# A hybrid decoder step on one core: pooling sums spread over the projection, pages loaded from SyncE, zero products at the start, and a separate first buffer between the expert passes

## The reference

```python
q, g, cmp_r, sel_r, win_r, u = project(x, norm1_g, w_in, q_norm_g, k_norm_g)
# rmsnorm(x) @ w_in; q and two of the keys are normalised per head of 64
kc, vc = compress(...)             # 32-token blocks of cmp rows through gelu(rows @ w1) @ w2
o = gated sum of compressed, selected-block and window attention
d = trailing_mean(u, w) - u        # w = 2, 4, 8, 16 for four groups of 128 channels
y = (d @ pool_w) * pool_scale      # one 128 x 128 map per group: the "mix"
h = x + concat(o, y) @ w_out
out = h + peer_ffn(rmsnorm(h))     # 16384 single-neuron experts, top 16 of each of 8 heads
```

## Time and profile before

| what | value |
|---|---|
| device time, median of 3 runs | 1684.33 us (1682.02 to 1684.73) |
| the profiled execution: time, span | 1685.28 us, 1683.6 us |
| mean granted TensorE clock | 0.992 |
| busy: PE, DVE, ACT, POOL | 1636.4, 1382.9, 754.5, 516.3 us |
| project: first and last product of PE | 7.12 us, 128.5 us |
| attend: first product of PE | 139.32 us |
| experts: first u unit, first v unit | 503.58 us, 1136.37 us |

### The profile page before, as it was taken

One profiled execution on the slowest core, in us unless ns is written; L12 is line 12 of the kernel. 1 busy time (PEld: TensorE's weight loads), 2 busy tenths in 40 slices (PEclk: granted clock), 3 DMA queues, 4 the chain that ended last, 5 costly groups with the idle time before them and its releaser, 6 DMA issues.

```text
span 1683.6 us, 29916 instructions
## 1 busy us (share of the span) xinstructions
PE 1636.4 (97%) x10496; PEld 1564.9 (93%) x10496; DVE 1382.9 (82%) x2831; ACT 754.5 (45%) x1423; POOL 516.3 (31%) x473
## 2 busy tenths in 40 slices
PE   7997999999999999999999999999999999999999
PEld 7985766689999999999999999999999999999999
DVE  5482456777889999999999989867998899999996
ACT  4331354453224334666666668733333333333332
POOL 3423222100001333322322343342443444444440
PEclk9997999999999999999999999999999999999999
DMA  7626233223226888888988899998999999999994
GB/s 233 209 79 187 76 99 108 78 70 113 64 76 201 286 303 317 290 322 302 330 319 317 304 341 345 361 386 312 354 390 342 366 386 402 398 393 395 401 394 143
DMA packets 187720, 454.20 MB, mean 270 GB/s; under 512 B 25666, under 2 KB 92098, under 8 KB 187106
## 3 DMA queue, kind: packets, MB, share of 16 engines
q1 hardware_dynamic: 111282, 242.78, 40.8%
q0 software_dynamic: 50272, 182.23, 29.5%
q10 hardware_dynamic: 26016, 27.27, 4.7%
HBM read 401.14 MB, written 54.47 MB: 271 GB/s over the span
## 4 chain that ended last, share of the span: by engine, by line
PE 61%; DVE 4%; DMA 3%; issue 1%; ACT 0%; SPq 0%; DVEq 0%; ACTq 0%; POOLq 0%
PE ps L2128 10%; PE ps L2124 10%; PE ps L2123 10%; PE ps L2152 9%; PE ps L2158 9%; PE ps L2155 9%; PE ps L2174 5%; DMA sb_ring<-expert_v 3%; DVE sb_w_lo L1953 1%; DVE sb_slot L1990 1%; DMA sb_scores<-expert_v,sb_row_expert 0%; DVE sb_rows_y L2085 0%; ACT sb_w_hi L1858 0%; DVE sb_hot L1989 0%; DVE sb_hot L1986 0%
## 5 line engine op out<-in xcount | busy, mean ns | idle before, releaser
L1858 ACT ACTIVATE sb_w_hi<-sb_ring 128x1024 fp32r<-128x1024 f32 x254 | 269.5, 1061 | 506.5 <-PE ps L2158 231.7
L1953 DVE TENSOR_TENSOR sb_w_lo<-sb_ring,sb_w_hi 128x1024 fp32r<-128x1024 f32 x255 | 312.1, 1224 | 63.3 <-ACT sb_w_hi L1858 61.9
L2123 PE MATMUL ps<-sb_x_hi,sb_w_hi 128*128 128x384 f32 x1024 | 349.9, 342 | 1.0 <-PEq L1346 1.0
L2124 PE MATMUL ps<-sb_x_lo,sb_w_hi 128*128 128x384 f32 x1024 | 345.4, 337 | 0.0
L2152 PE MATMUL ps<-sb_x_lo,sb_w_hi 128*128 128x384 f32 x1016 | 198.1, 336 | 6.4 <-ACT sb_x_lo L1867 6.4
L2128 PE MATMUL ps<-sb_x_hi,sb_w_lo 128*128 128x384 f32 x1024 | 201.1, 338 | 3.3 <-DVE sb_w_lo L1953 3.3
L2155 PE MATMUL ps<-sb_x_lo,sb_w_lo 128*128 128x384 f32 x1016 | 198.4, 337 | 0.0
L2158 PE MATMUL ps<-sb_x_lo,sb_w_hi 128*128 128x384 f32 x1016 | 197.6, 336 | 0.0
L2123 PEld LDWEIGHTS ps<-sb_x_hi,sb_w_hi 128*128 128x128 f32 x1024 | 191.9, 187 | 1.3 <-issue 1.3
L2124 PEld LDWEIGHTS ps<-sb_x_lo,sb_w_hi 128*128 128x128 f32 x1024 | 192.4, 188 | 0.0
L1848 POOL DMA_INDIRECT sb_scores<-expert_u_rows,sb_row_expert x80 | 100.4, 1255 | 295.0 <-DVE sb_row_dots L2074 208.1
(11 more groups left out here) (352 smaller groups left out, 2606.4 us busy)
## 6 DMA issues: line engine op xcount, KB each, us to landing
sb_ring<-expert_u SPq DMA_DIRECT2D x128, 512.0 KB, 5.8
sb_ring<-expert_v SPq DMA_DIRECT2D x128, 512.0 KB, 7.9
gates_dense<-sb_g_stage ACTq DMA_DIRECT2D x12, 2048.0 KB, 17.8
hid_dense<-sb_hid SPq DMA_DIRECT2D x104, 192.0 KB, 5.0
sb_scores<-hid_dense SPq DMA_DIRECT2D x104, 192.0 KB, 7.1
sb_g_stage<-gates_dense SPq DMA_DIRECT2D x32, 384.0 KB, 6.5
sb_g_stage<-gates_dense SPq DMA_DIRECT2D x48, 256.0 KB, 8.1
sb_ring<-peer_wq SPq DMA_DIRECT2D x16, 512.0 KB, 3.6
```

What stands on the lines that cost most here:

```text
L1858: nc.scalar.activation(whi[v % 2][:, :], ring(v)[:, :], ACT.Copy).then_inc(w_hi, 1)
L1953: nc.vector.tensor_tensor(wlo[v % 2][:, :], ring(v)[:, :], whi[v % 2][:, :], ALU.subtract).then_inc(w_lo, 1)
L2123: nc.tensor.matmul(out, hi[:, c * P:(c + 1) * P], g.x_hi[:, c], start=(c == 0), stop=False)
L2124: nc.tensor.matmul(out, hi[:, c * P:(c + 1) * P], g.x_lo[:, c], start=False, stop=False)
```

## The change

In `project`: POOL no longer copies u. ACT copies each of the tiles 10 to 13 into `ext` when it is out (`fill`), and DVE makes that group's sum soon after. The mixes leave `ITEMS`; they get banks 6 and 7, and stand behind tile 0, in the middle of tile 1, behind tile 1 and behind the gates. The mean over the channels moves into the middle of tile 10, the last head mean into the middle of tile 7, the first transposes behind tile 9. PE begins with 8 float32 products of zeros, which DVE writes. The second half of the first weights is split before x. SP issues all pages 0 to 31, behind the weights' loads of tiles index 10 to 13. In `attend`, SP and POOL issue only pages 32 to 63. In `experts`: the lo parts of units 2 to 6 are made by POOL; unit 0 of the v pass has a `chi` buffer of its own, and PE takes the bank of the last gelu last; the three moves and the sum go from units 34 and 37 to 106 and 110, and their store to the end.

```diff
-SP_PAGES = ((*EARLY_PAGES, 16, 17, 18), (15,), range(32, 48))
-POOL_PAGES = (range(19, 31), (31,), range(48, 64))
+PAGES_AT = {10: range(0, 5), 11: range(5, 10), 12: range(10, 19), 13: range(19, 32)}
+LATE_PAGES = 15
+SP_PAGES = range(32, 48)
+POOL_PAGES = range(48, 64)
...
-        ITEMS = [4, 5, 10, 11, 12, 13, 6, 8, 0, 1, "gates", 2, 3, "mix0", "mix1", "mix2", "mix3", 7, 9]
+        ITEMS = [4, 5, 10, 11, 12, 13, 6, 8, 0, 1, "gates", 2, 3, 7, 9]
...
-        place = lambda i: 6 if i == 2 else 2 * (i % 2) if i < 2 else 2 * ((i + 1) % 2)
+        place = lambda i: {2: 6, 3: 4}.get(i, 2 * (i % 2))
+        MIX_BANK = 6
+        WARM = 8
...
+                for k in PAGES_AT.get(t, ()):
+                    if k == 0:
+                        sp.wait_ge(g.rest_in, 16 * (1 + len(g.rest)))
+                        sp.wait_ge(diffed, 4)
+                    if k == LATE_PAGES:
+                        sp.wait_ge(cmp_mm, MIX_MM(3))
+                    load_page(sp, g, k).then_inc(g.page_in[0], 16)
...
-            pool.wait_ge(item_out, at[13] + 1)
-            pool.tensor_copy(ext[:, :, PST:NW], g.zT[:, ZT_U:NZT, 0:SEQ])
...
-            for k in POOL_PAGES[0]:
-                load_page(pool, g, k).then_inc(g.page_pool[0], 16)
...
+                    if kh == 0 and between:
+                        between()
...
+                if i == 3:
+                    pe.wait_ge(sq_ready, STD_READY)
+                elif i >= 4:
+                    pe.wait_ge(item_out, i - 3 if i < 6 else i - 1)
...
+            def mix(n):
+                pe.wait_ge(pool_in, 176)
+                pe.wait_ge(diffed, n + 1)
+                if n:
+                    pe.wait_ge(mix_out, n)
+                else:
+                    pe.wait_ge(cmp_dve, K_NORMED)
+                for h in range(2):
+                    last = nc.tensor.matmul(bank(g, MIX_BANK + h)[:, 0:HALF], pw[:, n], diff[:, n, h * HALF:(h + 1) * HALF], start=True, stop=True)
+                last.then_inc(cmp_mm, 1)
...
+            pe.wait_ge(x_lo_made, ZEROED)
+            for n in range(WARM):
+                nc.tensor.matmul(bank(g, 7)[:, 0:HALF], idle[:, 0:P], idle[:, P:P + HALF], start=True, stop=True)
+            BETWEEN = {10: mean_d, 1: lambda: mix(1), 7: lambda: head_mean(5)}
...
-            nc.scalar.activation(rk[:, 0:1], rk[:, 0:1], ACT.Square).then_inc(sq_ready, 1)
+            nc.scalar.activation(rk[:, 0:1], rk[:, 0:1], ACT.Sqrt).then_inc(sq_ready, 1)
...
+            def fill(k):
+                if k == 0:
+                    act.wait_ge(filled, POS_PLACED)
+                act.wait_ge(item_out, at[10 + k] + 1)
+                nc.scalar.activation(ext[:, k, PST:NW], g.zT[:, ZT_U + k, 0:SEQ], ACT.Copy)
+                nc.scalar.activation(exts(ext[:, k])[:, :, PST:SW_], g.zT[:, ZT_U + k, SEQ:T].rearrange("p (b n) -> p b n", b=DB), ACT.Copy).then_inc(filled, 1)
...
             # VectorE's order now
+            out(10)
+            out(11)
+            pool_group(0)
+            out(12)
+            pool_group(1)
...
+            pool_group(2)
...
+            out(13)
+            pool_group(3)
             out(6)
-            pool_group(0)
             out(8)
-            pool_group(1)
...
-        chi = [g.x_lo[:, k] for k in range(2)]
+        chi_first = sb("c_hi_first", [P, ND], F32R)
+        chi = lambda u: g.x_lo[:, u % 2] if u else chi_first[:, :]
...
-        MOVE_AT, SUM_AT, KEEP_AT = NKEY + 34, NKEY + 37, NKEY + 40
+        MOVE_AT, SUM_AT = NKEY + 106, NKEY + 110
...
+            def low_part(v):
+                pool.wait_ge(w_hi, v + 1 - AHEAD_U)
+                pool.wait_ge(mm, v - 1)
+                pool.tensor_tensor(wlo[v % 2][:, :], ring(v)[:, :], whi[v % 2][:, :], ALU.subtract).then_inc(lo_by_pool, 1)
+
+            for v in POOL_LO:
+                if v < FIRST_ROWS:
+                    low_part(v)
...
-                    if u == 0:
-
-                        act.wait_ge(mm, NU)
...
-                    pe.wait_ge(gelu, NU)
+                    pe.wait_ge(gelu, NU - 1)
...
+                last_u_bank = (NU - 1) % 2
+                for m in [m for m in range(KC) if m != last_u_bank] + [last_u_bank]:
+                    if u == 0 and m == last_u_bank:
+                        pe.wait_ge(gelu, NU)
+                    nc.tensor.matmul(out(m), hi[:, m * P:(m + 1) * P], chi(u), start=(u == 0), stop=False)
```

More of the change, by code:

```diff
@@ L289, in _, with tile @@
             halves_of = [slice(h * HALF, (h + 1) * HALF) for h in range(2)]
-            def tile(t, b):
+            def tile(t, b, between=None):
                 at_ = [bank(g, b + h)[:, 0:HALF] for h in range(2)]
@@ L314, in tile, with item @@
                     last.then_inc(item_mm, 1)
-            def item(i):
+                    if kh == 0 and between:
+                        between()
+            def item(i, between=None):
                 x = ITEMS[i]
                 b = place(i)
[L319 to L324, removed]
+                if i == 3:
+                    pe.wait_ge(sq_ready, STD_READY)
+                elif i >= 4:
+                    pe.wait_ge(item_out, i - 3 if i < 6 else i - 1)
                 if x == "gates":
@@ L333, in item, with mean_d @@
                     last.then_inc(item_mm, 2)
[L334 to L340, removed]
-                else:
-                    tile(TILES.index(x), b)
+                else:
+                    tile(TILES.index(x), b, between)
+            def mean_d():
+                pe.wait_ge(first_in, 32)
+                pe.wait_ge(sq_used, KC - 1)
+                for h in range(2):
+                    last = nc.tensor.matmul(bank(g, 4 + h)[:, 0:HALF], g.c["c_mean_d"][:, :], sq[:, 0, h * HALF:(h + 1) * HALF], start=True, stop=True)
+                last.then_inc(sq_used, 1)
+            def mix(n):
[5 more added lines that the diff above has]
+                    pe.wait_ge(cmp_dve, K_NORMED)
+                for h in range(2):
+                    last = nc.tensor.matmul(bank(g, MIX_BANK + h)[:, 0:HALF], pw[:, n], diff[:, n, h * HALF:(h + 1) * HALF], start=True, stop=True)
+                last.then_inc(cmp_mm, 1)
             def head_mean(n):
@@ L419, in square @@
                 tile = NORMED[n]
-                act.wait_ge(item_out, at[tile] + (1 if at[tile] < at["mix0"] else -3))
+                act.wait_ge(item_out, at[tile] + 1)
                 if n >= 2:
@@ L461, in _ @@
             square_x(1)
+            square_x(2)
             high_part(1, 1)
-            for k in range(2, KC):
+            for k in range(3, KC):
                 square_x(k)
             high_part(2, 0)
+            high_part(2, 1)
             act.wait_ge(first_in, 32)
@@ L479, in _ @@
             high_part(6, 1)
+            fill(3)
             act.wait_ge(cmp_dve, SUMMED)
@@ L512, in _ @@
             high_part(12, 1)
+            root(4)
+            square(5)
+            high_part(13, 0)
+            root(5)
+            high_part(13, 1)
             act.wait_ge(turn_mm, GATES_T)
@@ L871, in sub @@
                 if q % 16 == 0:
[L872 to L873 removed]
+                    pe.wait_ge(g.page_in[e], 16 * len(SP_PAGES) if e else 16 * 32)
+                    if e:
+                        pe.wait_ge(g.page_pool, 16 * len(POOL_PAGES))
                 if q % 4 == 0 and m >= 2:
@@ L1637 @@
 AHEAD_U = 2
+FIRST_ROWS = 7
 AHEAD_LO = 1
+POOL_LO = range(2, 7)
 def dense_step_unit(d):
@@ L1779, in experts @@
         used = {x: j + 1 for j, x in enumerate(order)}
+        by_pool = lambda v: sum(x < v for x in POOL_LO)
+        lo_of = lambda v: (lo_by_pool, by_pool(v) + 1) if v in POOL_LO else (w_lo, v + 1 - AHEAD_LO - by_pool(v))
         dots_at = [next(v for v in range(NV) if rows_done(v) >= used[("u", 8 * q + 7)]) for q in range(NR // 8)]
@@ L1850, in _ @@
                                         bounds_check=NKEY * NKEY - 1).then_inc(row_in[j % NROW], 16)
+                for v in POOL_LO:
+                    if v >= FIRST_ROWS and rows_done(v - 1) + NROW - 1 == j:
+                        low_part(v)
         @block.scalar
@@ L2095, in _ @@
             for v in range(NV):
-                if v + 1 < NV:
+                if v + 1 < NV and v + 1 not in POOL_LO:
                     prepare_weights(v + 1)
```

184 lines of the change are left out of this document (85 added, 99 removed).

## The result

The change saves 19.8 us: 1664.72 us (median of 4 executions, 1656.30 to 1666.54) against 1684.53 us (4 executions, 1682.02 to 1685.31), a ratio of 0.9874 with a 95% interval of 0.9851 to 0.9898. Forecast were 1659 us and a gain of 25.5.

What follows compares the result with a forecast made beforehand. PE, busy 97% of the span, was taken as the bound, so only its waits or slower clock give time back. 17.0 + 3.7 + 1.1 + 1.2 + 2.5 = 25.5 us, forecast 1659 us; own range 1656 to 1662, wide range 1650 to 1668.

Steps and rivals of the forecast that it cites:

- the block's end alone: End of project, half of rival 1: the block's end costs its 2.7 us instead of 0.3, +2.4 us.
- the first rival: End of project: clock falls all the same or block's end costs 2.7 us; +3.7 or +2.4, 1662.5 to 1665; chance 0.22.
- the third: Experts: v pass runs without stalls, 6.4 us saved instead of 2.5, giving 1655 us; chance 0.12.
- the better start: Start of project: better bound -0.5 us instead of the expected +0.3; with a stall-free v pass, 1653 us.
- End of block and project: Project's work ends 7.0 us earlier and attend follows 0.3 us behind the last work: attend begins 17.0 us earlier.
- Clock: Start of attend: PE's shorter pause keeps granted clock at 1.00 instead of 0.50, saving 3.7 us, lower bound 0.
- the other change of blocks: Support for the clock gain: a window there with 3.58 of 5 us of PE work was granted 1.00.
- u pass: Experts: POOL makes lo parts for units 2 to 6, so the 1.13 us pause before L2128 goes; 1.1 us.
- The price of up to 3 us a part: Rule against it: POOL's five lo parts slow DVE through shared SBUF interfaces, up to 5 x 3 us in u pass.
- Change of passes: Experts: other chi buffer lets ACT copy during last u unit; 1.21 us pause at 1136.37 goes; 1.2 us (0.5 to 1.2).
- v pass: Experts: moving moves and sum to unit 106 regains 2.5 of 6.4 us lost (bounds -2 and +6.4).
- The second rival: Experts: v pass stalls only move; 2.5 us lost, perhaps 2 more, 1661.5 to 1663.5; chance 0.15.

## Why the prediction was right, and where it was off

The forecast of 25.5 us was made of five terms; these are their sizes in the spans of the profiled executions, 20.5 us in all. The forecast adds up as written. Two rivals do not: the block's end alone (2.4 us) gives 1661.4 us, which the first rival's 1662.5 to 1665 leaves out, and the third with the better start gives 1654, not 1653. The 0.7 us of L578 are in the trace (693 ns the shortest), not in the earlier trace rows.

- **End of block and project, 17.0 forecast, 18.1 measured.** The work ended 8.2 us earlier (7.0 forecast), and 10.0 us came from the end of the block, as forecast. Pauses, mixes, pages on SP and the 0.3 us between the last work and attend came as the rows said. The start was taken at 0.3 us lost, from the view that tile 0 ends on the lo chain; item 1 starts 0.1 us earlier instead, and the run without zeros shows that the zero products bought 1.3 us of this. Right in sum, wrong in that reason. The sums did run beside PE without a pause of it.
- **Clock, 3.7 forecast, 2.1 measured.** Attend's first product to the first u unit took 364.26 us before and 362.12 after. The first rival came partly true: the clock fell all the same, only later and for a shorter time. The argument from the other change of blocks, with 1.00 at 3.58 of 5 us, does not carry over: here 4.55 and 4.12 of 5 us were followed by 0.71. The Trainium skill, "TensorE: Matmul & The Clock Gate", Part 1, says that the slow state is the default and activity releases it; the run with three more products, with 5.00 and 4.64 of 5 us and 1.00 behind them, agrees.
- **u pass, 1.1 forecast, 1.2 measured** (631.24 us from the start of its first product to the start of its last, then 630.06). POOL's lo parts took 2.5 us each, a little under the estimate. DVE slowed beside them: one of its two bf16 products L2035 took 3.31 us and the other 1.23, where in before both took 1.23, and PE did not wait for it. The trace so agrees with the Trainium skill, "GPSIMD Engine Reference", Key points, on the interfaces that the two engines share. The price of up to 3 us a part that the prediction set against it did not come.
- **Change of passes, 1.2 forecast, -1.3 measured.** This step failed. It took ACT's wait for the end of the u pass as the only thing that holds `chi`. The row of before shows ACT's copy just behind that end, but there are two other inputs. In before the gates' last piece landed 1.6 us and the weights 3.6 us ahead of that end; in after the gates landed 1.2 us behind it and the weights 0.7 us ahead. What moved their landing was not found.
- **v pass, 2.5 forecast, -0.3 measured.** The pauses shrank by 4.1 us, more than forecast, but for no reason of the change: with the moves at 34 they were as small. The second rival, that they only move, is nearest to what the runs show: the pauses of the v pass are 5.0 to 7.2 us with the moves at 106 (seven traces) and 5.1 and 5.9 us with them at 34. And the pitch cost 4.4 us, a term that the sum lacked; it was to be seen in the trace of before, where u units take 4.24 us at 700 us and v units 4.16 at 1400.

The last 0.6 us lie outside these terms, most of it behind the v pass. The predicted range held because the terms of project carry most of the gain, and they were read from brackets. The forecast's own range (1656 to 1662) missed the first median by 2.7 us; the pitch alone differs by up to 7.5 us between the v passes of the table. That the range of 1650 to 1668 held for every execution of the first session is partly luck: two terms of 3.7 us together gave a loss of 1.6 in the profiled one, and a later execution of the same program took 1668.71 us.

## What to carry to other kernels

Before a pause is counted as gain, look at every input of the waiting instruction, and by how much each is ahead, in more than one trace: here the weights were 3.6 us ahead in one and 0.7 us in the next, and the pause stayed. Moving work from one saturated stretch to another gave nothing here. And when a block's last stretch is thin in products, a few spare ones in a free bank can be worth more than they cost: here 0.4 us of delay against 3.7 and 4.7 us less at the first u unit.

## What was not expected of the hardware

- **Three pitches.** Products of 384 columns with a weight load each start 173.33, 174.67 or 176.67 ns apart at a granted clock of 1.00 (in the second case 171 to 178 ns by turns), where 384 columns at 2.4 GHz would be 160 ns, one column a cycle (an estimate). It holds over hundreds of products and can change at each pause of PE, even of 0.05 us; a unit of the v pass is 4.16, 4.19 or 4.24 us by it, and the pass up to 7.6 us longer. In the u pass, behind the products of the gating matrices (from about 650 us), it was 176.7 ns nearly throughout in every trace, so there it does go with the place in the program. What in the chip sets it was not found. The Trainium skill, "TensorE: Matmul & The Clock Gate", Part 1, gives 2.5 ns above the columns' time for products back to back; an estimate by it is 162.5 ns, and the measurement decides: 11 to 14 ns more.
- **A wait for itself** costs PE 0.39 us, and was followed by the fast pitch 123 times in 126.
- **The clock's later falls.** Which stretches of attend get 0.50 differs between executions of one program: the changed kernel had them at 124, 165 and 200 us in two traces, and at 122, 241 and 333 us in another, 10.2 and 13.7 us in all. With three products more between 118.8 and 121.2 us only one fall was left, near 238 us, in both traces, and the first u unit came 4.7 and 3.7 us earlier. What a fall costs depends on where it lies: with 10.2 us of half clock the first u unit came at 483.3 us, and with 13.7 at 482.3.
